# Score matmuls with a contraction of 64: the two row halves of the array in turn

## The reference, cut to what matters

```python
# retention, 4 heads, dk = 64, dv = 128, chunks of 64 tokens
scores = einsum('bcnhd,bcmhd->bchnm', qc, kc) * intra_decay
o_intra = einsum('bchnm,bcmhe->bcnhe', scores, vc)
...
# differential attention, 4 heads, two groups j of 64 channels in each head
sc = einsum('bqhjd,bkhjd->bhjqk', qb, k) * scale
p = masked_softmax_2(sc, chunk_causal_mask(i, s))
w = p[:, :, 0] - lam * p[:, :, 1]
o = einsum('bhqk,bkhe->bqhe', w, v)
```

## Time and profile before

| | |
|---|---|
| median of 3 runs | 2127.25 us |
| profiled execution, its own time | 2127.4 us |
| its span, first to last instruction | 2125.6 us |
| TensorE busy (matmul) | 2095.3 us, 99% |
| weight loads busy | 1799.6 us, 85% |
| VectorE busy | 1413.3 us, 66% |
| ScalarE busy | 1050.3 us, 49% |
| mean granted TensorE clock | 0.999 |

### The profile page before, as it was taken

How to read it: one execution, slowest core, us unless ns; L and a number is a source line. 1 busy time by engine, 2 the same in 40 slices (tenths; PEclk the granted TensorE clock), 3 DMA queues, 4 the chain that set the end, 5 groups by cost and what they waited for, 6 DMA issues and landing times.

```text
span 2125.6 us, 27729 instructions
## 1 busy us (share of the span) xinstructions
PE 2095.3 (99%) x11559; PEld 1799.6 (85%) x11559; DVE 1413.3 (66%) x1802; ACT 1050.3 (49%) x1520; POOL 106.2 (5%) x121
## 2 busy tenths in 40 slices
PE   8999999999999999999999999999999999999998
PEld 7989888989888888887888888888888878888887
DVE  5657876657877766665675566675766667655655
ACT  5344646444645555545454454554544454444543
POOL 0100010010010010000000000000100000000000
PEclk9999999999999999999999999999999999999999
DMA  8353245453235665444554465565644545544552
GB/s 284 112 199 128 94 136 180 122 199 125 95 123 203 209 217 172 164 139 159 178 181 157 149 216 189 198 208 184 212 156 159 158 159 178 184 173 151 194 184 96
DMA packets 193271, 357.24 MB, mean 168 GB/s; under 512 B 8381, under 2 KB 85369, under 8 KB 193146
## 3 DMA queue, kind: packets, MB, share of 16 engines
q1 hardware_dynamic: 190410, 345.51, 48.7%
q0 software_dynamic: 2736, 9.96, 1.3%
HBM read 354.40 MB, written 1.05 MB: 167 GB/s over the span
## 4 chain that ended last, share of the span: by engine, by line
PE 79%; DVE 3%; ACT 1%; issue 0%; DMA 0%; POOL 0%; DVEq 0%; ACTq 0%
PE bank L2029 14%; PE bank L2033 14%; PE bank L2039 14%; PE bank L2071 12%; PE bank L2075 6%; PE bank L2093 2%; PE bank L2084 2%; PE bank L2053 2%; PE bank L2056 2%; PE bank L2059 2%; PE bank L2110 1%; PE bank L2213 1%; DVE raw_r L2538 1%; PE bank L2101 1%; PE bank L2296 1%; PE bank L2131 1%
## 5 line engine op out<-in xcount | busy, mean ns | idle before, releaser
L2538 DVE TENSOR_TENSOR raw_r<-raw,high 128x2048 fp32r<-128x2048 f32 x304 | 686.3, 2267 | 78.4 <-ACT high L2322 77.2
L2322 ACT ACTIVATE high<-raw 128x2048 fp32r<-128x2048 f32 x304 | 575.5, 1897 | 228.2 <-PE bank L2039 173.0
L2029 PE MATMUL bank<-high,units_r 128*128 128x512 f32 (+1 forms) x1576 | 628.8, 399 | 4.4 <-ACT high L2322 3.0
L2033 PE MATMUL bank<-high,units_r 128*128 128x512 f32 (+1 forms) x1576 | 615.3, 390 | 2.0 <-DVE units_r L2562 1.1
L2039 PE MATMUL bank<-raw_r,units_r 128*128 128x512 f32 (+1 forms) x1576 | 423.4, 389 | 0.0
L2029 PEld LDWEIGHTS bank<-high,units_r 128*128 128x128 f32 x1576 | 296.8, 188 | 65.5 <-issue 4.0
L2033 PEld LDWEIGHTS bank<-high,units_r 128*128 128x128 f32 x1576 | 297.0, 188 | 61.3 <-DVE units_r L2559 2.2
L2039 PEld LDWEIGHTS bank<-raw_r,units_r 128*128 128x128 f32 x1576 | 296.1, 188 | 62.3 <-DVE raw_r L2538 0.7
L2071 PE MATMUL bank<-units_r,high 128*128 128x512 f32 x1152 | 288.2, 392 | 0.0
L2071 PEld LDWEIGHTS bank<-units_r,high 128*128 128x128 f32 x1152 | 208.4, 189 | 38.1
L2075 PEld LDWEIGHTS bank<-units_r,raw_r 128*128 128x128 f32 x1152 | 157.2, 190 | 11.2
(11 more groups left out here) (262 smaller groups left out, 2207.2 us busy)
## 6 DMA issues: line engine op xcount, KB each, us to landing
raw<-in_ffn_w_dram SPq DMA_DIRECT2D x132, 1024.0 KB, 5.1
raw<-in_w_in_dram SPq DMA_DIRECT2D x108, 1024.0 KB, 5.1
raw<-in_w_out_dram SPq DMA_DIRECT2D x24, 1024.0 KB, 4.9
raw<-in_cross_wkv_dram SPq DMA_DIRECT2D x16, 1024.0 KB, 5.2
raw<-in_w_branch_dram SPq DMA_DIRECT2D x12, 1024.0 KB, 4.9
raw<-in_cross_wq_dram SPq DMA_DIRECT2D x8, 1024.0 KB, 5.4
raw<-in_cross_wo_dram SPq DMA_DIRECT2D x8, 1024.0 KB, 4.9
raw<-in_w_in_dram SPq DMA_DIRECT2D x4, 832.0 KB, 4.5
```

Source lines behind the costliest of these rows:

```text
L2029: pe.matmul(o, h.high(k0 + k)[:, span], p.hi[k][:, cols], start=start and k == 0, stop=False, skip_group_check=True)
L2033: pe.matmul(o, h.low(k0 + k)[:, span], p.hi[k][:, cols], start=False, stop=False, skip_group_check=True)
L2322: done = act.activation(high, raw, ACT.Copy)
L2538: done = dve.tensor_tensor(low, raw, high.bitcast(F32), ALU.subtract)
```

## The change

Differential attention calls scores_pair once for each query tile, in place of scores once for each group. It takes both units and both banks at once, and TensorE's new tile scores_of_two issues the matmuls of head 0 group 0, head 0 group 1, head 1 group 0 and so on, so that neighbours lie in different halves of the array's rows and go to different banks. One semaphore increment stands behind both groups' matmuls of a step. The two yields of 4 become one of 8. What each call adds to plan.work is n * L * 4 for both groups together. Retention's loops are turned round: first the whole rectangles of both i in turn (ret_two), then the second key tiles of both i in turn. That adds 2048 and 1024 to plan.work. VectorE's, ScalarE's and the later steps are as they were, but behind each other in the new order: the evacuations of both groups, and then the maxima and exponentials of both.

```diff
@@ -653,6 +653,25 @@
             self.do("scores", name=name, need=need, q=q, n=n, L=L, of=of, steps=steps, bank=bank, u=u, p3=p3,
                     bias=bias, scale=scale)
             self.B.give(bank, ("scored", name, q))
+        return self.soft(name, u, p3, nh, q, exp)
+
+    def scores_pair(self, names, need, nh, L, ofs, bias, scale):
+
+
+        per = 512 // max(L, 128)
+        units = [self.U.take() for _ in names]
+        p3s = [u.ap[:, 0:nh * L].rearrange("p (h l) -> p h l", h=nh) for u in units]
+        for q in range(0, nh, per):
+            n = min(per, nh - q)
+            banks = [self.B.take() for _ in names]
+            self.work += n * L * 4
+            self.do("scores_of_two", names=names, need=need, q=q, n=n, L=L, ofs=ofs, banks=banks)
+            for name, bank, u, p3 in zip(names, banks, units, p3s):
+                self.do("scores", name=name, q=q, n=n, L=L, bank=bank, u=u, p3=p3, bias=bias, scale=scale, of=None)
+                self.B.give(bank, ("scored", name, q))
+        return [self.soft(name, u, p3, nh, q, True) for name, u, p3 in zip(names, units, p3s)]
+
+    def soft(self, name, u, p3, nh, q, exp):
         mx, sm = self.st(nh), self.st(nh)
         self.do("soft_max", name=name, p3=p3, mx=mx, scored=("scored", name, q))
         if exp:
@@ -1634,15 +1653,14 @@
 
             def tile(t):
                 L = P * (t + 1)
-                got = []
-                for jj in range(2):
-                    def of(i, j, jj=jj):
-                        return (h3(qT.ap[64 * jj:64 * jj + 64, :], 4)[:, i, t * P:t * P + P],
-                                h3(kT.ap[64 * jj:64 * jj + 64, :], 4)[:, i, 0:L])
-
-                    got.append(plan.scores(f"{N}.ds{t}{jj}", t_made, 4, L, of, 1, cst("chunk")[:, 256 - L:256],
-                                           64.0 ** -0.5))
-                    yield 4
+
+                def of(jj, i):
+                    return (h3(qT.ap[64 * jj:64 * jj + 64, :], 4)[:, i, t * P:t * P + P],
+                            h3(kT.ap[64 * jj:64 * jj + 64, :], 4)[:, i, 0:L])
+
+                got = plan.scores_pair([f"{N}.ds{t}{jj}" for jj in range(2)], t_made, 4, L, of,
+                                       cst("chunk")[:, 256 - L:256], 64.0 ** -0.5)
+                yield 8
                 (u1, p1, s1, soft1), (u2, p2, s2, soft2) = got
                 D = f"{N}.dd{t}"
                 do("diff_mix", name=D, need=[soft1, soft2], p1=p1, s1=s1, p2=p2, s2=s2, L=L, l=l, lam=lamt[:, l:l + 1])
@@ -1689,12 +1707,13 @@
             s0, s1 = U.take(), U.take()
             r3 = h3(rT.ap, 4)
             s_made = []
-            for i in range(2):
-                for whole in (True, False):
-                    R = f"{N}.rs{i}{int(whole)}"
-                    b = B.take()
-                    plan.work += 2 * (256 if whole else P) * 4
-                    do("ret_scores", name=R, need=t_made, r3=r3, i=i, whole=whole, bank=b, dst=s0 if whole else s1)
+            for whole in (True, False):
+                RS = [f"{N}.rs{i}{int(whole)}" for i in range(2)]
+                bs = [B.take(), B.take()]
+                plan.work += 2 * (256 if whole else P) * 4
+                do("ret_two", names=RS, need=t_made, r3=r3, whole=whole, banks=bs)
+                for i, (R, b) in enumerate(zip(RS, bs)):
+                    do("ret_scores", name=R, i=i, whole=whole, bank=b, dst=s0 if whole else s1)
                     B.give(b, ("decayed", R))
                     s_made.append(("decayed", R))
             U.give(rT, ("ret_scores", R))
@@ -2084,7 +2103,19 @@
             turned = pe.transpose(bank.ap[:, i * P:i * P + P], src[:, k * P:k * P + P], ident)
         turned.then_inc(*mark(s.turned, ("turnp", name, q)))
 
-    def scores(name, need, q, n, L, of, steps, bank, **_):
+    def scores_of_two(names, need, q, n, L, ofs, banks, **_):
+        for e in (*need, *banks[0].after, *banks[1].after):
+            hold.wait_ge(*at(e))
+        for i in range(n):
+            for jj, bank in enumerate(banks):
+                left, right = ofs(jj, q + i)
+                score = pe.matmul(bank.ap[:, i * L:i * L + L], left, right, start=True, stop=True,
+                                  skip_group_check=True)
+        score.then_inc(*mark(s.attn, *[("scores", name, q) for name in names]))
+
+    def scores(name, q, n, L, of, bank, need=None, steps=None, **_):
+        if of is None:
+            return
         for e in (*need, *bank.after):
             hold.wait_ge(*at(e))
         for i in range(n):
@@ -2261,18 +2292,19 @@
             turned = pe.transpose(bank.ap[0:96, i * P:i * P + P], src[:, 4 * g + i, :], ident)
         turned.then_inc(*mark(s.turned, ("mla_turn", name)))
 
-    def ret_scores(name, need, r3, i, whole, bank, **_):
-        for n in (*need, *bank.after):
-            hold.wait_ge(*at(n))
-        half = slice(64 * i, 64 * i + 64)
+    def ret_two(names, need, r3, whole, banks, **_):
+        for n in (*need, *banks[0].after, *banks[1].after):
+            hold.wait_ge(*at(n))
         for q in range(2):
-            if whole:
-                score = pe.matmul(bank.ap[:, q * 256:q * 256 + 256], r3[half, 2 + q, 0:P], r3[half, q, :], start=True,
-                                  stop=True, skip_group_check=True)
-            else:
-                score = pe.matmul(bank.ap[:, q * P:q * P + P], r3[half, 2 + q, P:256], r3[half, q, P:256], start=True,
-                                  stop=True, skip_group_check=True)
-        score.then_inc(*mark(s.attn, ("ret_scores", name)))
+            for i, bank in enumerate(banks):
+                half = slice(64 * i, 64 * i + 64)
+                if whole:
+                    score = pe.matmul(bank.ap[:, q * 256:q * 256 + 256], r3[half, 2 + q, 0:P], r3[half, q, :], start=True,
+                                      stop=True, skip_group_check=True)
+                else:
+                    score = pe.matmul(bank.ap[:, q * P:q * P + P], r3[half, 2 + q, P:256], r3[half, q, P:256], start=True,
+                                      stop=True, skip_group_check=True)
+        score.then_inc(*mark(s.attn, *[("ret_scores", name) for name in names]))
 
     def ret_v(name, need, t, s0, s1, rv, bank, **_):
         for n in (*need, *bank.after):
...
```

More of the change, by code:

```diff
@@ L2302, in tensor_program @@
                  hgrn_v=hgrn_v, latent_turn=latent_turn, mla_q=mla_q, mla_kv=mla_kv, mla_turn=mla_turn,
-                 ret_scores=ret_scores, ret_v=ret_v, cross_v=cross_v)
+                 ret_two=ret_two, scores_of_two=scores_of_two, ret_v=ret_v, cross_v=cross_v)
     for kind, how in steps:
```

## The result

The changed kernel takes 2118.81 us (median of 5 runs, 2118.66 to 2121.36) against 2126.35 us before (5 runs). The ratio is 0.9966 with a 95% interval of 0.9954 to 0.9977: 5 to 10 us faster. The profiled executions are 2127.4 and 2118.81 us, with spans of 2125.6 and 2117.0 us: 8.6 us, against 8.7 forecast.

A forecast was written before the change was run, and what follows sets the result against it. TensorE, busy for 2095.3 of 2125.6 us, bounds the kernel. Gains of 3.40 (differential attention) and 0.93 (retention) in each of two layers, 8.7 us, bring 2127.4 to 2118.7, 2118.6 as a median; range 2116.0 to 2123.0 us.

The forecast's parts named there:

- The visits: Scores after the change: differential attention's t0 visit 1.16 us, t1 visit 2.12, retention 1.70; gains 3.40 and 0.93 a layer.
- One sign of the forecast: Differential attention's timeline: groups 0 and 1 start within 0.02 us of each other, pairs 0.22 us apart at t1, 0.11 at t0.
- accidental overlap in retention: Kernel before: a lower-half record starts 0.01 us behind an upper one; for a third of a microsecond neither stream slowed the other.
- rivals 1 and 2: Paired halves overlap only in part (2122.4 us, chance 0.14) or not at all, switches alone gained (2126.4 us, chance 0.05).
- switches and retention's lost overlap: Without any overlap: 0.80 us a layer gained in differential attention, 0.37 lost in retention, together 0.9 us for both layers.
- rival 3: VectorE's and ScalarE's doubled chains make splits late and TensorE waits for weights: 2134.1 us, chance 0.04.
- the zero price: VectorE's longer chain behind the t1 scores makes a split 2.9 us late, hidden by 8.4 us spare: price 0.
- The planner: Retention's step counts 3072, not 6144, so one more tok is drawn in; differential attention begins at the same place: 0 us.

The follow-up runs named there:

- the kernel on the upper half alone: Changed kernel with both groups, and both halves of retention, reading partitions 0 to 63, banks still alternating: 2125.87 us, ratio 0.9995 to the kernel before.
- old count: Changed kernel with retention's two steps adding 4096 and 2048 to the planned work, the total before the change: 2116.14 us, ratio 0.9954 to the kernel before.
- the kernel with the halves one after the other: Changed kernel with all upper-half matmuls of each step issued first, then all lower-half ones: 2120.73 us, ratio 0.9970 to the kernel before.

## Why the prediction was right

*The bound.* Nearly all of TensorE's time is work, so time taken from it came off the end: 8.66 us in the two stages, 8.6 in the span.

*The visits.* The same reading as in the forecast gives, for t0, 976.93 - 0.23 - 975.50 = 1.20 us (forecast 1.16), for t1, 989.98 - 0.46 - (986.71 + 1.07 - 0.39) = 2.13 (2.12), and for retention, (898.67 - 0.23) - (895.84 + 1.05 - 0.27 + 0.11) = 1.71 (1.70). By these terms the gain is 3.35 + 0.92 = 4.27 a layer; I had 3.40 + 0.93. One sign of the forecast held only in part: I had said that the two groups start within 0.02 us of each other. At t1 it is 0.007 us, but at t0 it is 0.04 from the second pair on, and these are the 0.04 us by which t0 costs more.

*Overlap.* The forecast rested on 0.3 us of accidental overlap in retention. It was evidence enough: the pairs run at the full pace of each stream, which also refutes rivals 1 and 2. What I called an accident followed a rule in every order run here: a queued matmul for the other half started once no more than three records of the busy half were still to start (blocks of two, four and eight records).

*The split of the gain.* The forecast's own figures said 0.9 us for switches and retention's lost overlap together and 7.8 us for the overlap; the kernel on the upper half alone gives 0.41 + 0.47 and 3.91 + 3.87.

*VectorE's chain (rival 3).* VectorE's timeline of the changed kernel, behind the t1 scores:
```profile
988.89 2.48 DVE L2633 SCALAR_TENSOR_TENSOR units<-bank,consts 128x512 f32<-128x512 f32 x4 [2.25 <-PE bank L2112]
991.29 1.21 DVE L2638 TENSOR_REDUCE stat<-units 128x4 f32<-128x1024 f32 x1
...
992.61 1.21 DVE L2638 TENSOR_REDUCE stat<-units 128x4 f32<-128x1024 f32 x1
...
993.94 2.28 DVE L2570 TENSOR_TENSOR raw_r<-raw,high 128x2048 fp32r<-128x2048 f32 x1
```
The chain is 5.05 us long, where the old one was 2.93; I had said 5.8. The difference lies in the evacuations: before, two of them took 1.59 us up to the maxima (998.57 to 1000.16), with a wait of 0.17 us for the second bank between them, and now four take 2.40. By the same count of splits and low products the least spare time near here fell from 8.4 to 6.1 us. That is the margin that carried the zero price. The 1.7 us that this rival added to each delay has no row behind it, and no run shows it: no split became late.

*The planner.* The order came out as followed on paper: a tok between retention's scores and the transposes, differential attention from the same place on, four toks behind each pair. The old count shows the shift to be worth 0.07 us.

*Time.* Forecast 2118.6, measured 2118.81 us. That the two agree to 0.2 us is in part luck. The term of the sum, 8.7 us, is confirmed by the stages (8.66), but what lies outside the stages moves a run by 2 to 3 us either way, and the kernel with the old count, with nearly the same stages, has a median of 2116.14.

## What to carry to other kernels

Where TensorE is full, matmuls with a contraction of 64 should go to both halves of the rows in turn, into different banks. Here that halved the time in which they stream, and because TensorE looked past three queued records, blocks of four records a half came within 0.1 us a visit of strict alternation.
## What the runs showed that I had not expected

The look past three records, with its exact count, and that the switch costs the same 0.38 to 0.40 us for a form of 15 rows as for 64.

And two reasons why single runs scatter by 1 to 3 us. The first is stretches of TensorE at the lower of its two clock levels (1.2 GHz for 2.4), at a place that differs from run to run. Stage view, 140 to 155 us, of the kernel with the halves one after the other and then of the changed kernel; the columns are length, busy times with counts of PE, PEld, DVE, ACT and POOL, granted clock, DMA share and GB/s:
```profile
140.00:155.00 15.00, 13.14 (x66) 10.98 (x65) 9.13 (x18) 8.37 (x8) 2.14 (x1) 0.82 0.87 323
```
```profile
140.00:155.00 15.00, 13.04 (x77) 10.57 (x75) 11.05 (x20) 9.20 (x10) 2.69 (x1) 1.00 0.91 342
```
The code is the same up to there, yet the first one got through 66 records and the second through 77, at a mean granted clock of 0.82 against 1.00. The second 96-row landmark then came at 897.89 against 895.84 us. Ahead of such stretches TensorE had been waiting; between 140 and 150 us even the undisturbed run is busy for only 8.0 of 10 us. Which run gets the slower stretch nothing in the kernel decides, as far as I can see, and why it falls where it does stays open.

The second reason is the start of the program. The timelines of TensorE of the changed kernel and then of the kernel with the old count, whose code is the same here:
```profile
17.32 1.47 PE L2103 MATMUL bank<-consts,units 128*128 128x128 f32 x8
...
561.38 2.02 PE L2222 MATMUL bank<-units 128*128 128x128 f32 x16 [1.00 <-ACT units L2518]
```
```profile
16.70 1.03 PE L2103 MATMUL bank<-consts,units 128*128 128x128 f32 x8
...
558.74 2.02 PE L2222 MATMUL bank<-units 128*128 128x128 f32 x16 [0.55 <-ACT units L2518]
```
The same eight transposes take 1.47 us in one run and 1.03 in the other, and by 20 us the changed kernel is 1.1 us behind. At 561 it is 2.64 behind, as it alone had a slower stretch between 538 and 562 us (mean granted clock 0.93 against 1.00), and the first landmark of the stage shows the same 2.66 (895.84 and 893.18). That is nearly all of the 2.7 us by which their medians differ; the two stages together differ by 0.12 us.
